# A two-layer hybrid decoder step with product-key experts: openings of PSUM banks, an inverse, sums of squares and the causal mixers rewritten with fewer and smaller products

## The chip, the cores and the metric

One of the eight cores of a Trainium2 chip runs the kernel. The metric is the device time of one launch in microseconds (us), from the first to the last instruction with what lies around them. All data is float32, in which TensorE (PE) runs each product as two records in the trace, a load of the stationary operand and a pass of the moving one each time. Transposes run as one.

## What is computed

A prompt of 256 tokens and 8 samples of one token (264 columns) go through two layers of the same form. `xn` is the normalised input.

```python
proj = xn @ w_in                        # 4 mixers' columns, then 4 x 1024 gate columns
y_a = rwkv7(proj)                       # per head a 64x64 state, delta rule
y_b = hgrn2(proj)                       # gated linear attention
y_c = retention(proj)                   # causal scores times a decay
y_d = mlstm(proj)                       # causal scores times exp(gates), with a normaliser
merged = sum(sigmoid(gates_m) * (y_m @ w_branch_m) for m in range(4))
x = x + merged @ w_out
q = rms_norm(x) @ peer_w_q              # 8 heads, two halves against 128 keys each
i1, i2 = top16(q1 . keys1), top16(q2 . keys2)
eidx, gate = top16 of the 256 sums, softmax     # 128 experts per token
x = x + sum(gate * gelu(u[eidx] . xn) * v[eidx])
```

Retention and mLSTM need for every head, with q, k and v of 64 channels, `att = (q k^T) * mask`, then `att v` and (mLSTM) the sums of the rows of `att`. RWKV-7 is done in chunks of 64 tokens: its update needs the inverse of `I + M` for each chunk and head, where `M` is strictly triangular, 64x64; there are 16 of them (4 chunks, 4 heads).

## The kernel before

The work is written out by hand for five engines, which meet at semaphores; the order on each engine is the order in the code. Channels lie on the partitions and tokens in the free dimension. Per layer:

- **Input products** (L503 to L551, `column_tile`): 32 column tiles of the mixers' part of `w_in`, 8 products of 128x128 by 264 columns each. HGRN2's own work (products `head_sum`, transposes, a scan) is set between them; after tile 25 comes its last sum into bank 6, opened and closed by a product of zeros (`nothing`) with 512 columns (L543, L551), which starts or ends the accumulation.
- **Mixers**: RWKV-7 first. `chunk_m` gets the chunks' matrices; the inverse (L651 to L663 on PE, L1431 to L1442 on VectorE, DVE) starts from the identity in `xx` and runs 6 rounds with blocks of 1, 2, 4 ... 32; each round is a product `T` (L654), a masking on DVE (`rr`), two products (L660, L662) and an addition. `open_y` (L640) opens the two banks of the outputs with 512 columns of zeros, L668 the bank of the states; then a chain of 4 chunks. Then retention and mLSTM by `causal(mixer, ...)` (L699 to L748), between them the two scalar gates of mLSTM (L757 to L760, `w_if`), once for each gate with 4 stationary columns.
- 32 **gate tiles** (`gate_products`, L566; again 8 products of 264 columns) are spread over the mixers as filling, by the constants `EARLY_GATES`, `GATES_AT` and others. Weights come in blocks of 1 MB (2 tiles) through four slots of `ring`, by SP's queue.
- **Branches, output projection** (`project`, L838) and query projection (L857). In `project`, DVE adds every block to `x` (L1642) and squares it (L1288); PE sums the squares over the partitions with a product by ones, two blocks later (`sum_square`, L485). ScalarE's root (L948), DVE's reciprocal and the norm follow.
- **Experts**: for each of 2 token tiles 128 gathers of 128 rows of 8 KB (POOL, L1262), for the samples 8. DVE makes the dot product (L1737), ScalarE the gelu and a diagonal matrix (L1171, L1173), PE the weighted sum (`weighted`, L893), into two banks that `open_sum` (L899) and `close_sum` (L903) open and close with 512 columns of zeros each. At the end ScalarE copies the sums (L1183), PE turns them, DVE adds them to `x`.

In `causal` PE transposes values and keys (L705), ScalarE copies them (`vpad`, `ktok`), POOL copies the keys of each head into `keyz` (L1226), which is zero in the other head's 64 rows, so that a product with all 128 rows (L714, L715) gives one head's scores:

```python
mm(bank(b, SEQ), keyz[:, mixer, q, pr, 0:P], q_[:, pr, 0:SEQ], start=True, stop=True)
mm(bank(b, P, SEQ), keyz[:, mixer, q, pr, P:SEQ], q_[:, pr, P:SEQ], start=True, stop=True).then_inc(S("pe_sc"), 1)
```

The values stand in `vpad` between 64 columns of zeros on each side, so that the products of both heads of a pair (L725, L727) add up in all 128 partitions of one bank. The sums of mLSTM's rows use `onespad` in the same way.

## Time and profile before

| | |
|---|---|
| median of 3 runs | 2353.87 us (2351.02 to 2362.21) |
| the profiled execution | 2362.78 us, its span 2360.7 us |
| mean granted TensorE clock | 0.933 |
| PE busy | 1984.7 us (84%) |
| DVE busy | 1418.6 us (60%) |
| ScalarE (ACT) busy | 583.7 us (25%) |
| GpSimd (POOL) busy | 651.4 us (28%) |
| moved by DMA | 665.61 MB, mean 282 GB/s |

The span runs from the first to the last instruction. The durations of a stretch are those of this one execution. The granted clock is a share of full speed (2.4 GHz); of a stretch it is a mean over its two levels, 1.2 and 2.4 GHz. "PEld" is PE's loading of stationary operands, which can run beside its passes. A shape such as "128*128 128x264" is stationary rows * columns, then what moves.

### The profile page before, as it was taken

What the parts mean: (1) busy time and instruction counts of PE and PEld (TensorE: products, weight loads), DVE (VectorE), ACT (ScalarE), POOL (GpSimd) and SP (SyncE); (2) the same over time, 40 slices, a digit from 0 to 9 for tenths busy, and PEclk for the clock granted to TensorE, in tenths of its full rate; (3) what the DMA queues carried; (4) which work ended last, traced back from release to release, by engine and by line L of the source; (5) the groups of instructions that cost most, each with busy time, mean ns of one, the idle gap of its engine ahead of it and who ended that gap; (6) DMA issues with size and microseconds to landing.
All of it is one profiled execution on the core that took longest, in us unless ns stands there. A gap on an engine that the chain in (4) does not pass through costs nothing.

```text
span 2360.7 us, 25431 instructions
## 1 busy us (share of the span) xinstructions
PE 1984.7 (84%) x7872; PEld 1176.3 (50%) x7872; DVE 1418.6 (60%) x3591; ACT 583.7 (25%) x1556; POOL 651.4 (28%) x668
## 2 busy tenths in 40 slices
PE   6999989997778877878889898899878878777887
PEld 5767677763333332323368677787433333333323
DVE  1425454458878777776533443644687786877755
ACT  1221222033222222222222203220332222322222
POOL 0400000024444444544213000000434444344441
PEclk9999989999888998899999999999988989898998
DMA  6330233559999999999853201433899999999995
GB/s 238 122 109 2 75 117 113 191 195 422 396 421 416 415 421 409 412 422 410 355 204 108 91 36 42 153 126 143 341 402 416 421 414 410 421 417 415 415 422 218
DMA packets 102051, 665.61 MB, mean 282 GB/s; under 512 B 20240, under 2 KB 21936, under 8 KB 21936
## 3 DMA queue, kind: packets, MB, share of 16 engines
q0 software_dynamic: 76032, 553.68, 57.0%
q1 hardware_dynamic: 24208, 107.12, 12.7%
q10 hardware_dynamic: 1696, 3.46, 0.4%
q8 instruction: 50, 0.82, 0.1%
q14 instruction: 65, 0.53, 0.1%
HBM read 657.64 MB, written 6.58 MB: 281 GB/s over the span
## 4 chain that ended last, share of the span: by engine, by line
PE 49%; DMA 26%; DVE 14%; issue 6%; ACT 3%; POOL 1%; SPq 0%; POOLq 0%; DVEq 0%; another core or an unknown queue 0%; ACTq 0%
DMA arena<-in_uv,arena 25%; PE ps L893 17%; PE ps L505 9%; PE ps L566 6%; PE ps L857 3%; PE ps L824 2%; PE ps L838 2%; DVE ring L1737 1%; PE ps L485 1%; ACT arena L1173 1%; POOL arena L1262 1%; PE ps L759 1%; PE ps L515 1%; DVE arena L1667 1%; DVE arena L1660 1%
## 5 line engine op out<-in xcount | busy, mean ns | idle before, releaser
L893 PE MATMUL ps<-ring,arena 128*128 128x512 f32 x1056 | 563.3, 688 | 224.9 <-ACT arena L1173 224.8
L893 PE MATMUL ps<-arena 128*128 128x512 f32 x1056 | 487.8, 602 | 46.6 <-ACT arena L1173 46.5
L893 PEld LDWEIGHTS ps<-ring,arena 128*128 128x128 f32 x1056 | 225.2, 221 | 560.4 <-ACT arena L1173 325.2
L1737 DVE SCALAR_TENSOR_TENSOR arena<-arena 128x1024 f32<-128x1024 f32 x264 | 323.3, 1225 | 222.3 <-DMA arena<-in_uv,arena 222.3
L1262 POOL DMA_INDIRECT ring<-in_uv,arena x264 | 296.5, 1123 | 469.4 <-PE ps L893 423.2
L1737 DVE SCALAR_TENSOR_TENSOR ring<-ring,arena 128x1024 f32<-128x1024 f32 x264 | 322.4, 1221 | 125.7 <-DMA ring<-in_uv,arena 91.4
L893 PEld LDWEIGHTS ps<-arena 128*128 128x128 f32 x1056 | 192.1, 189 | 334.7 <-issue 194.5
L1262 POOL DMA_INDIRECT arena<-in_uv,arena x264 | 273.2, 1035 | 247.2 <-PE ps L893 197.9
L1171 ACT ACTIVATE arena<-arena 128x1 f32<-128x1 f32 x528 | 107.1, 203 | 910.0 <-DVE ring L1737 487.8
L566 PE MATMUL ps<-xn,ring 128*128 128x264 f32 x1024 | 251.7, 406 | 15.7 <-ACTq L1122 9.3
L505 PE MATMUL ps<-xn,ring 128*128 128x264 f32 x1024 | 236.3, 391 | 6.0 <-DVE xn L1295 6.0
L566 PEld LDWEIGHTS ps<-xn,ring 128*128 128x128 f32 x1024 | 202.4, 200 | 55.6 <-issue 18.4
L1173 ACT ACTIVATE arena<-arena 128x128 f32<-128x128 f32 x528 | 212.5, 402 | 32.9 <-ACT arena L1171 2.0
L505 PEld LDWEIGHTS ps<-xn,ring 128*128 128x128 f32 x1024 | 196.3, 193 | 46.2 <-DVE xn L1295 6.9
L1738 DVE TENSOR_SCALAR arena<-const,arena 128x128 f32<-128x128 f32 x528 | 149.1, 282 | 0.0
L1252 POOL COPY arena<-arena 128x8 uint32 (+1 forms) x66 | 23.5, 356 | 402.6 <-DVEq L1716 402.3
L1226 POOL COPY keyz<-arena 64x512 f32<-64x512 f32 x8 | 4.9, 609 | 376.8 <-DVEq L1483 286.1
L967 ACT ACTIVATE arena<-ps 128x264 f32<-128x264 f32 x64 | 25.3, 395 | 224.8 <-PE ps L505 224.7
L1014 ACT ACTIVATE arena<-ps 128x264 f32<-128x264 f32 x50 | 19.6, 391 | 214.0 <-PE ps L566 213.7
L857 PE MATMUL ps<-xn,ring 128*128 128x264 f32 x256 | 61.1, 395 | 5.9 <-DVE xn L1295 5.9
L1236 POOL TENSOR_TENSOR arena<-arena 128x480 f32<-128x480 f32 (+14 forms) x30 | 28.3, 942 | 134.8 <-DVEq L1332 132.6
L824 PE MATMUL ps<-arena,ring 128*128 128x264 f32 x256 | 57.5, 387 | 2.0 <-remote 2.0
(391 smaller groups left out, 1794.9 us busy)
## 6 DMA issues: line engine op xcount, KB each, us to landing
ring<-in_w SPq DMA_DIRECT2D x88, 1024.0 KB, 4.9
ring<-in_uv,arena POOLq DMA_INDIRECT x264, 10.4
arena<-in_uv,arena POOLq DMA_INDIRECT x264, 14.0
st<-in_st SPq DMA_DIRECT2D x2, 2048.0 KB
out_st<-st SPq DMA_DIRECT2D x2, 2048.0 KB
const<-in_const ACTq DMA_DIRECT2D x1, 2729.0 KB, 11.5
arena<-in_keys SPq DMA_DIRECT2D x2, 1024.0 KB, 6.8
x<-in_x SPq DMA_DIRECT2D x1, 1056.0 KB, 5.2
```

Of the source, the lines that this page charges most:

```text
L505: m = mm(bank(b), ring[:, j, at:at + P], xn[:, kt, :], start=kt == 0, stop=kt == KT - 1)
L566: m = mm(bank(b), ring[:, j, at:at + P], xn[:, kt, :], start=kt == 0, stop=kt == KT - 1)
L824: m = mm(bank(b), ring[:, j, at:at + P], yy[:, 2 * m_ + k, :], start=k == 0, stop=k == 1)
L838: m = mm(bank(6 + o % 2), ring[:, j, at:at + P], src[:, kt, :], start=kt == 0, stop=kt == KT - 1)
L857: m = mm(bank(6 + o % 2), ring[:, o // 2, at:at + P], xn[:, kt, :], start=kt == 0, stop=kt == KT - 1)
L893: m = mm(bank(2 * tt + half, 512), dg[:, k, :], row(k)[:, D + 512 * half:D + 512 * half + 512], start=False, stop=False, skip_group_check= ...
L1171: own(act(hge[:, k:k + 1], hid[:, k:k + 1], ACT.Gelu))
L1173: act(dg[:, k, :], gd[:, k, :], ACT.Copy, scale=hge[:, k:k + 1]).then_inc(S("act_dg"), 1)
L1236: tt_(pairs[j], before[:, :, :, 1:], sub(HG + 2)[:, :, :, 1:SUB + 1 - j], ALU.mult).then_inc(S("pool_hg"), 1)
L1262: e.indirect_dma_start(out=row(k), out_offset=None, in_=A["uv"], in_offset=bass.IndirectOffsetOnAxis(ap=ix[:, par, k:k + 1], axis=0)).then ...
L1737: stt(u, u, 1.0, xtok[:, tt, :], ALU.mult, ALU.mult, accum_out=hid[:, k:k + 1]).then_inc(S("dve_hid"), 1)
L1738: ts(gd[:, k, :], C("ident"), gate, None, ALU.mult).then_inc(S("dve_hid"), 1)
```

## The change

1. **Openings.** The last sum of HGRN2 is opened by a product of zeros over 32 columns and closed by its own last product. `open_y` covers only the half of the columns which the following products don't write themselves. L668, `open_sum` and `close_sum` use one column, and `close_sum` one product instead of two.
2. **Inverse.** The first round, with blocks of 1, is `I` plus masked elements of `chunk_m`. DVE makes the transposed one by a masking with the new constant `level0` and an addition, PE turns it by a product with the identity (`channel`), DVE copies it. Five rounds follow.
3. **Causal mixers.** `keyz`, `vpad`, `onespad` and POOL's copies are gone. Scores of both heads of a pair are products over 64 rows each, `q = 0` and `q = 1` next to each other, into banks 6 and 7. Values lie dense in `vals`; the products with them have 64 stationary columns and write 64 partitions each.
4. **Scalar gates.** `w_if` gets 36 columns (4, 28 of zeros, 4), so that one pass makes both gates.
5. **Squares.** In `project` DVE adds up the eight squares itself, and PE makes one product by ones at the end.

The constants are 128 columns shorter. Input and output are the same otherwise.

```diff
@@ -540,7 +539,8 @@
                                        vexp[:, tt, h, :, :].rearrange("p c v -> p (c v)"), start=True, stop=True)
                         m.then_inc(S("pe_step"), 1)
                     if t == 25:
-                        mm(bank(6, 512), nothing, const[:, 0:512], start=True, stop=False, skip_group_check=True)
+                        mm(bank(6, 512).rearrange("p (a b) -> p a b", b=SEQ)[:, :, 0:SUB], nothing, nothing[:, 0:PR * SUB].rearrange("p (a b) -> p a b", b=SUB),
+                           start=True, stop=False, skip_group_check=True)
                         for c in range(1, NSUB):
                             e.wait_ge(S("dve_hs"), c)
                             for h in range(H):
@@ -548,7 +548,7 @@
                                 ch = slice(HD * q, HD * q + HD)
                                 m = mm(ps[ch, 6, pr * SEQ + c * SUB:pr * SEQ + c * SUB + SUB], hst[ch, pr, c - 1, :],
                                        eb[ch, pr, c * SUB:c * SUB + SUB], start=False, stop=False, skip_group_check=True)
-                        mm(bank(6, 512), nothing, const[:, 0:512], start=False, stop=True, skip_group_check=True).then_inc(S("pe_step"), 1)
+                        m.then_inc(S("pe_step"), 1)
                 e.wait_ge(S("sp_ln"), 16)
                 e.wait_ge(S("sp_par"), 16 * 8)
 
...
                 def open_y(u):
 
-                    mm(bank(1 + u, 512), nothing, const[:, 0:512], start=True, stop=False, skip_group_check=True)
+                    mm(bank(1 + u, 512).rearrange("p (a b) -> p a b", b=2 * CH)[:, :, chunk(1 - u)], nothing, bc(nothing[:, 0:CH], 1, [P, 4, CH]), start=True, stop=False, skip_group_check=True)
                     for tt in range(TT):
                         for h in range(H):
                             pr, q = divmod(h, 2)
@@ -647,14 +647,19 @@
 
                 open_y(0)
 
-                for k in range(6):
+                for tt in range(TT):
+                    e.wait_ge(S("dve_inv"), tt + 1)
+                    for h, u, on, n in heads_of(tt):
+                        m = mm(ps[on, 5 + tt, h * CH:h * CH + CH], xx[on, tt, 1, h, :], C("channel")[on, :], start=True, stop=True)
+                    m.then_inc(S("pe_p"), 1)
+                for k in range(1, 6):
                     for tt in range(TT):
-                        e.wait_ge(S("dve_inv"), max(2 * k + tt, 1))
+                        e.wait_ge(S("dve_inv"), 2 * k + tt + 1)
                         for h, u, on, n in heads_of(tt):
                             m = mm(ps[on, 3 + tt, h * CH:h * CH + CH], chunk_m[on, n, 0:CH], xx[on, tt, 0, h, :], start=True, stop=True)
                         m.then_inc(S("pe_t"), 1)
                     for tt in range(TT):
-                        e.wait_ge(S("dve_r"), 2 * k + tt + 1)
+                        e.wait_ge(S("dve_r"), 2 * k + tt - 1)
                         if k < 5:
                             for h, u, on, n in heads_of(tt):
                                 mm(ps[on, 5 + tt, h * CH:h * CH + CH], xx[on, tt, 1, h, :], rr[on, tt, h, :], start=True, stop=True)
@@ -664,8 +669,8 @@
 
                 e.wait_ge(S("act_step"), step("act_bv"))
                 open_y(1)
-                e.wait_ge(S("dve_inv"), 13)
-                mm(bank(6, 512), nothing, const[:, 0:512], start=True, stop=False, skip_group_check=True)
+                e.wait_ge(S("dve_inv"), 14)
+                mm(bank(6, 1), nothing, nothing[:, 0:1], start=True, stop=False, skip_group_check=True)
                 open_banks(7, 0)
                 for c in range(NCH):
                     tt, u = divmod(c, 2)
...
 
-                def causal(mixer, q_, k_tiles, v_tiles):
+                def causal(mixer, q_, k_, v_tiles):
 
 
                     e.wait_ge(S("dve_qk"), mixer + 1)
...
                     m.then_inc(S("pe_ctr"), 1)
                     close_banks(6, 7)
-                    e.wait_ge(S("pool_kz"), mixer + 1)
-                    for h in range(H):
-                        pr, q = divmod(h, 2)
-                        b = 6 + h % 2
-                        if h >= 2:
-                            e.wait_ge(S("dve_att"), 4 * mixer + h - 1)
-                        mm(bank(b, SEQ), keyz[:, mixer, q, pr, 0:P], q_[:, pr, 0:SEQ], start=True, stop=True)
-                        mm(bank(b, P, SEQ), keyz[:, mixer, q, pr, P:SEQ], q_[:, pr, P:SEQ], start=True, stop=True).then_inc(S("pe_sc"), 1)
+                    for pr in range(PR):
+                        if pr:
+                            e.wait_ge(S("dve_att"), 4 * mixer + 2)
+                        for q in range(2):
+                            mm(bank(6 + q, SEQ), k_[chunk(q), pr, 0:P], q_[chunk(q), pr, 0:SEQ], start=True, stop=True)
+                        for q in range(2):
+                            mm(bank(6 + q, P, SEQ), k_[chunk(q), pr, P:SEQ], q_[chunk(q), pr, P:SEQ], start=True, stop=True).then_inc(S("pe_sc"), 1)
                     e.wait_ge(S("act_cv"), mixer + 1)
                     e.wait_ge(S("dve_att"), 4 * mixer + 4)
                     e.wait_ge(S("dve_y"), 1)
-                    def over_keys(out, late, values):
-
-                        for q, tt in ((0, 0), (0, 1), (1, 1), (1, 0)):
-                            h = 2 * pr + q
-                            pad = HD - HD * q
-                            if tt:
-                                m = mm(late, values(tt, h, pad), att[:, h, SEQ:ATT], start=False, stop=False, skip_group_check=True)
-                            else:
-                                m = mm(out, values(tt, h, pad), att[:, h, 0:SEQ], start=q == 0, stop=q == 1)
+
+                    def over_keys(b, values):
+
+                        for pr in range(PR):
+                            for q in range(2):
+                                mm(ps[chunk(q), b + pr, 0:SEQ], values(0, 2 * pr + q), att[:, 2 * pr + q, 0:SEQ], start=True, stop=False)
+                            for q in range(2):
+                                m = mm(ps[chunk(q), b + pr, P:SEQ], values(1, 2 * pr + q), att[:, 2 * pr + q, SEQ:ATT], start=False, stop=True)
                         return m
 
-                    for pr in range(PR):
-                        m = over_keys(bank(pr, SEQ), bank(pr, P, P), lambda tt, h, pad: vpad[:, tt, h, pad:pad + P])
+                    m = over_keys(0, lambda tt, h: vals[:, tt, h * HD:h * HD + HD])
                     if mixer:
-                        a = CONST_AT["onespad"][0]
-                        for pr in range(PR):
-                            m = over_keys(bank(2 + pr, SEQ), bank(2 + pr, P, P), lambda tt, h, pad: const[:, a + pad:a + pad + P])
+                        m = over_keys(2, lambda tt, h: C("ones", HD))
                     m.then_inc(S("pe_co"), 1)
 
                     e.wait_ge(S("dve_kw"), mixer + 1)
...
                 causal(0, qr, kq, proj[:, RT + 4:RT + 6, :])
-                for g in range(2):
-                    for kt in range(KT):
-                        m = mm(ps[0:4, 2 + g, 0:N], w_if[:, kt, 4 * g:4 * g + 4], xn[:, kt, :], start=kt == 0, stop=kt == KT - 1)
+                for kt in range(KT):
+                    m = mm(ps[0:36, 2, 0:N], w_if[:, kt, :], xn[:, kt, :], start=kt == 0, stop=kt == KT - 1)
                 m.then_inc(S("pe_step"), 1)
...
                         m.then_inc(S(tag), 1)
-                        if o >= 2:
-                            sum_square(2, o - 2)
-                    for kt in range(KT - 2, KT):
-                        sum_square(2, kt)
+                    e.wait_ge(S("dve_sq"), KT + 1)
+                    mm(bank(2), C("ones"), sqs2[:, 0, :], start=True, stop=True).then_inc(S("pe_ss"), 1)
 
                 project(merged, "pe_wo", "dve_x")
 
...
                 def open_sum(tt):
                     for half in range(2):
-                        mm(bank(2 * tt + half, 512), nothing, const[:, 0:512], start=True, stop=False)
+                        mm(bank(2 * tt + half, 1), nothing, nothing[:, 0:1], start=True, stop=False, skip_group_check=True)
 
                 def close_sum(tt):
-                    for half in range(2):
-                        m = mm(bank(2 * tt + half, 512), nothing, const[:, 0:512], start=False, stop=True)
-                    m.then_inc(S("pe_acc"), 1)
+                    mm(bank(2 * tt + 1, 1), nothing, nothing[:, 0:1], start=False, stop=True, skip_group_check=True).then_inc(S("pe_acc"), 1)
...
                 e.wait_ge(S("act_step"), step("act_sv0"))
-                e.tensor_copy(xx.rearrange("p a b c d -> p (a b c) d"), bc(C("channel"), 1, [P, TT * 2 * H, CH])).then_inc(S("dve_inv"), 1)
-                for k_ in range(6):
+                for tt in range(TT):
+                    e.wait_ge(S("dve_cm"), 2 * tt + 2)
+                    own(tt_(xx[:, tt, 1, :, :], chunk_m[:, tt * H:tt * H + H, 0:CH], bc(C("level0"), 1, [P, H, CH]), ALU.mult))
+                    tt_(xx[:, tt, 1, :, :], xx[:, tt, 1, :, :], bc(C("channel"), 1, [P, H, CH]), ALU.add).then_inc(S("dve_inv"), 1)
+                for tt in range(TT):
+                    e.wait_ge(S("pe_p"), tt + 1)
+                    e.tensor_copy(xx[:, tt, 0, :, :].rearrange("p a b -> p (a b)"), bank(5 + tt, 256)).then_inc(S("dve_inv"), 1)
+                for k_ in range(1, 6):
                     lev = CONST_AT["levels"][0] + k_ * CH
                     for tt in range(TT):
-                        e.wait_ge(S("pe_t"), 2 * k_ + tt + 1)
+                        e.wait_ge(S("pe_t"), 2 * k_ + tt - 1)
                         tt_(rr[:, tt, :, :], bank(3 + tt, 256).rearrange("p (a b) -> p a b", b=CH), bc(const[:, lev:lev + CH], 1, [P, H, CH]), ALU.mult)\
                             .then_inc(S("dve_r"), 1)
                     for tt in range(TT):
...
-                    square(o, sqs2)
+                    own(tt_(sqs2[:, o, :], x[:, o, :], x[:, o, :], ALU.mult))
+                    if o:
+                        own(tt_(sqs2[:, 0, :], sqs2[:, 0, :], sqs2[:, o, :], ALU.add))
+                e.sem_inc(S("dve_sq"), 1)
 
                 norm(2, lambda kt: V("ln2", kt))
```

Three places show how the change moves instructions. Each row is an instruction with its line, output and inputs and, in brackets, the semaphores that it waits for; "x8" is eight alike in a row.

PE from the opening of the y banks to the first rounds of the inverse (`dve_inv` comes when DVE has finished `xx`, `dve_r` when it has masked `rr`), before:

```order
L640 MATMUL ps<-const 128x512
L645 MATMUL ps<-arena 64x64 x8
L654 MATMUL ps<-arena 64x64 [waits dve_inv]
L654 MATMUL ps<-arena 64x64 x7
L654 MATMUL ps<-arena 64x64 [waits dve_inv]
L654 MATMUL ps<-arena 64x64 x7
L660 MATMUL ps<-arena 64x64 [waits dve_r]
L660 MATMUL ps<-arena 64x64 x7
L662 MATMUL ps<-arena 64x64 x8
L660 MATMUL ps<-arena 64x64 [waits dve_r]
```

and in the changed kernel:

```order
L640 MATMUL ps<-const 128x4x64
L645 MATMUL ps<-arena 64x64 x8
L653 MATMUL ps<-const,arena 64x64 [waits dve_inv]
L653 MATMUL ps<-const,arena 64x64 x7
L653 MATMUL ps<-const,arena 64x64 [waits dve_inv]
L653 MATMUL ps<-const,arena 64x64 x7
L659 MATMUL ps<-arena 64x64 [waits dve_inv]
L659 MATMUL ps<-arena 64x64 x7
L659 MATMUL ps<-arena 64x64 [waits dve_inv]
L659 MATMUL ps<-arena 64x64 x7
L665 MATMUL ps<-arena 64x64 [waits dve_r]
L665 MATMUL ps<-arena 64x64 x7
```

The products T (L654) that began the first round are replaced by products with the identity from `const` (L653); then the second round's T (now L659) waits for DVE's copies.

PE in a causal mixer, from the scores to the products with the values (`dve_att` counts the heads that DVE has masked, `pool_kz` POOL's copy, `act_cv` ScalarE's), before:

```order
L714 MATMUL ps<-arena,keyz 128x256 [waits pool_kz]
L715 MATMUL ps<-arena,keyz 128x128
L714 MATMUL ps<-arena,keyz 128x256
L715 MATMUL ps<-arena,keyz 128x128
L714 MATMUL ps<-arena,keyz 128x256 [waits dve_att]
L715 MATMUL ps<-arena,keyz 128x128
L714 MATMUL ps<-arena,keyz 128x256 [waits dve_att]
L715 MATMUL ps<-arena,keyz 128x128
L727 MATMUL ps<-arena,vpad 128x256 [waits dve_y,dve_att,act_cv]
L725 MATMUL ps<-arena,vpad 128x128 x2
L727 MATMUL ps<-arena,vpad 128x256 x2
L725 MATMUL ps<-arena,vpad 128x128 x2
L727 MATMUL ps<-arena,vpad 128x256
```

and in the changed kernel:

```order
L717 MATMUL ps<-arena 128x256 x2
L719 MATMUL ps<-arena 128x128 x2
L717 MATMUL ps<-arena 128x256 [waits dve_att]
L717 MATMUL ps<-arena 128x256
L719 MATMUL ps<-arena 128x128 x2
L728 MATMUL ps<-arena,vals 64x256 [waits dve_y,dve_att,act_cv]
L728 MATMUL ps<-arena,vals 64x256
L730 MATMUL ps<-arena,vals 64x128 x2
L728 MATMUL ps<-arena,vals 64x256 x2
L730 MATMUL ps<-arena,vals 64x128 x2
```

POOL is not waited for any more. There were two waits for a masked head between the scores, one for each later head; now there is one, which asks for two heads, ahead of both later heads.

PE in the output projection, its last two blocks (`dve_x` counts DVE's additions to `x`, `dve_sq` its squares), before:

```order
L838 MATMUL ps<-arena,ring 128x264 [waits dve_x]
L838 MATMUL ps<-arena,ring 128x264 x7
L485 MATMUL ps<-arena,const 128x264 [waits dve_sq]
L838 MATMUL ps<-arena,ring 128x264 [waits dve_x]
L838 MATMUL ps<-arena,ring 128x264 x7
L485 MATMUL ps<-arena,const 128x264 [waits dve_sq] x3
```

and in the changed kernel:

```order
L837 MATMUL ps<-arena,ring 128x264 [waits dve_x]
L837 MATMUL ps<-arena,ring 128x264 x7
L837 MATMUL ps<-arena,ring 128x264 [waits dve_x]
L837 MATMUL ps<-arena,ring 128x264 x7
L840 MATMUL ps<-arena,const 128x264 [waits dve_sq]
```

The sums of squares between and behind the blocks (L485) are gone but for one at the end (L840).

## Rows read from the trace of the kernel before

**Rows 1.** Stretches: start:end, length, busy time (records) of each engine, clock, DMA share, GB/s.

```profile
165.00:402.00 237.00, 212.94 (x1628) 169.83 (x1628) 110.89 (x210) 60.19 (x122) 2.44 (x4) 0.92 0.22 75
272.00:303.00 31.00, 30.23 (x118) 24.57 (x117) 14.26 (x47) 11.49 (x28) 1.23 (x2) 0.83 0.10 35
...
517.00:1170.00 653.00, 521.31 (x1068) 210.25 (x1068) 486.72 (x1296) 181.66 (x550) 289.36 (x287) 0.91 1.00 414
```

**Rows 2.** Chain that ended last, by engine (the page).

```profile
PE 49%; DMA 26%; DVE 14%; issue 6%; ACT 3%; POOL 1%; SPq 0%; POOLq 0%; DVEq 0%; another core or an unknown queue 0%; ACTq 0%
```

**Rows 3.** In order of time (start, length, instruction xrecords), gates and the gate tiles after.

```profile
262.39 7.28 PE L759 MATMUL ps<-xn,w_if 128*4 128x264 f32 x32
...
271.81 19.75 PE L566 MATMUL ps<-xn,ring 128*128 128x264 f32 x80 [2.13 <-ACTq L1083]
...
1435.52 18.06 PE L566 MATMUL ps<-xn,ring 128*128 128x264 f32 x80 [2.13 <-ACTq L1083]
```

**Rows 4.** In order of time, end of the experts in layer 1.

```profile
1177.34 1.88 PE L903 MATMUL ps<-const 128*128 128x512 f32 x4
...
1179.26 1.08 ACT L1183 ACTIVATE arena<-ps 128x512 f32<-128x512 f32 x2 [2.82 <-PE ps L903]
```

**Rows 5.** In order of time, loads for the one-column products (L746) of mixer 1.

```profile
313.45 0.97 PEld L746 LDWEIGHTS ps<-const,arena 128*128 128x128 f32 x8
```

**Rows 6.** In order of time, openings of the y banks in layer 1.

```profile
202.15 2.07 PE L640 MATMUL ps<-const 128*128 128x512 f32 x2
...
224.23 1.12 PE L640 MATMUL ps<-const 128*128 128x512 f32 x2
...
225.29 0.68 PE L645 MATMUL ps<-arena 64*64 64x64 f32 x16
```

**Rows 7.** In order of time, first round of the inverse in layer 1.

```profile
200.60 0.68 DVE L1432 COPY arena<-const 128x1024 f32<-128x1024 f32 x1
...
204.86 0.31 PE L654 MATMUL ps<-arena 64*64 64x64 f32 x1
...
206.71 0.63 PE L662 MATMUL ps<-arena 64*64 64x64 f32 x16
207.18 0.63 PE L660 MATMUL ps<-arena 64*64 64x64 f32 x16
...
208.13 0.68 PE L654 MATMUL ps<-arena 64*64 64x64 f32 x16
```

**Rows 8.** In order of time, products and loads in half of the array.

```profile
121.12 3.65 PE L539 MATMUL ps<-arena 128*64 128x512 f32 x16
...
122.03 0.14 PEld L539 LDWEIGHTS ps<-arena 128*64 128x64 f32 x2 [0.29 <-issue]
...
167.57 0.78 PE L585 MATMUL ps<-arena,wa_up 64*128 64x264 f32 x1 [3.34 <-ACT arena L1021]
...
167.57 0.80 PE L586 MATMUL ps<-arena,wa_up 64*128 64x264 f32 x1
```

**Rows 9.** In order of time, mixer 1 (mLSTM) in layer 1.

```profile
303.16 0.69 PE L714 MATMUL ps<-arena,keyz 128*128 128x256 f32 x2
...
304.47 1.02 DVE L1491 TENSOR_TENSOR arena<-ps,arena 128x384 f32<-128x384 f32 x2
...
307.36 0.67 PE L727 MATMUL ps<-arena,vpad 128*128 128x256 f32 x2 [0.70 <-issue]
...
312.67 1.05 PE L741 MATMUL ps<-vpad,arena 128*128 128x128 f32 x8
```

**Rows 10.** In order of time, last blocks of the output projection in layer 1.

```profile
457.63 0.61 PE L485 MATMUL ps<-arena,const 128*128 128x264 f32 x2
...
461.64 1.86 PE L485 MATMUL ps<-arena,const 128*128 128x264 f32 x6
461.84 0.43 DVE L1642 TENSOR_TENSOR x<-x,ps 128x264 f32<-128x264 f32 x1 [3.11 <-PE ps L838]
...
463.54 0.48 ACT L948 ACTIVATE arena<-ps,const 128x264 f32<-128x264 f32 x1 [60.38 <-PE ps L485]
```

60 lines of the change are left out of this document (20 added, 40 removed).

## The prediction

> **What bounds the kernel now.** I read the stages first [rows 1], then the chain of waits [rows 2], then the order of time in the places that the change touches. Layer 1 is ahead of the experts up to 517 us and in them up to some 1180 [rows 1]; layer 2 repeats it. In the experts' stage the DMA share is 1.00 at 414 GB/s and PE is busy 521 of 653 us [rows 1]: the gathered rows set the time, and PE's work there counts only after the last gather. Ahead of the experts PE is busy 213 of 237 us in the mixers [rows 1], and PE and DMA (nearly all of it the gathers) lead the chain with 49% and 26% [rows 2]. The first gathers wait for PE's projections, so what PE saves ahead of them moves the whole stage of the experts earlier. So I look for products on PE's own path; work that moves to DVE costs only where PE waits for DVE.
>
> **The change part by part**, for one layer, in us. A product in f32 is two records in the trace; 40 products of 264 columns took 18.06 at full clock [rows 3], 0.45 each, so 512 columns cost 0.86. Two such (L903) and the hand-over took 1.92 [rows 4], which agrees. A product of one column still loads 128 weights: eight such loads took 0.97 [rows 5], so the two of a product make 0.24.
>
> *Banks opened by one column.* After column tile 25 two products of 512 columns go and one of 32 comes, in the middle of a run of PE work: 2 x 0.86 - 0.24 = **1.5**. The second opening of the y banks halves its columns (0.43), and the opening of the state bank (L668) falls to one column: 0.86 - 0.24 = 0.62; both stand on the path to the chunk chain [rows 6]: **1.05**. In the experts, four openings and closings between the token tiles cost PE some 3.4, but DMA is at 1.00 through the stage [rows 1] and covers them, so I cost their going at nothing: without that cover it would be worth up to 3.4. The last closing stands bare: two products from 1177.34, ScalarE starts at 1179.26 [rows 4]; one column in their place saves 1.72 - 0.24 = **1.5**. Bounds for a one-column product: 0.12 (one load seen, the other hidden) to 0.5 (nothing pipelined), so the three sites, 4.05 together, lie between 3.1 and 4.5.
>
> *Shorter inverse.* Six rounds become five; in place of the first stand two masked additions per token tile on DVE, a product by the identity on PE and a copy. The first round ran from 204.86 to 208.13 [rows 7], 3.27. DVE is free at 200.60, where its copy of 0.68 stood [rows 7]; four operations of 256 columns, each some 0.45 with its wait, end at 202.4, while PE is still at the y opening (202.15) [rows 6]: hidden. That opening ran at half clock (2.0 for one product), and half of it goes: 0.86. PE then reaches the new product at about 204.1, issues 16 records in 0.47 (206.71 to 207.18 [rows 7]), DVE copies in 0.43 (264 columns out of PSUM [rows 10]), and with two hand-overs of 0.2 round 1 starts at 205.4 and not at 208.13: **2.7**, and 2.3 in layer 2, where the opening ran at full clock. Bounds 1.5 to 3.3.
>
> *Causal mixers.* Out goes POOL's copy and the padding. A score product now has 64 rows and its neighbour the other 64. That such pairs run side by side is seen at L585 and L586: both start at 167.57 and take 0.78 and 0.80 [rows 8]. But DVE masks head by head, and the second pair now waits for both heads of the first, where before head 2 waited for head 0 alone. In mixer 1 the old order took 303.16 to 307.36 [rows 9]. In the new, DVE still starts at 304.47, masks two heads in 1.02, PE needs 0.65 and a hand-over of 0.3, DVE 1.1 more: 307.75, so **-0.4**. In mixer 0 POOL's copy no longer gates (0.3) and half-clock products pair up: between 0.6 and -0.1, I take 0.
>
> The products with the values run in columns 0 to 63 and 64 to 127 together. L539 has this form: 8 products of 64x512 took 3.65, where 8 x 0.86 = 6.9 would be serial [rows 8]. Mixer 1 has 16 of these, 8 of 256 columns (0.43) and 8 of 128 (0.215), 5.2 in all (307.36 to 312.67 = 5.3 [rows 9]); half goes, **2.6**. Mixer 0 has 8: **1.3**. Against this, the array now changes shape twice on the path per mixer. From L640 to L645, where it changes, 1.06 passed and 0.86 is the product [rows 6]: 0.2 each time, so **-0.8** for both mixers.
>
> A rule speaks against this step. The Trainium skill, "TensorE: Matmul & The Clock Gate", Part 3, says that a weight load overlaps a running product only where the row groups differ, and these neighbours share all rows. L539's neighbours share them as well: its loads of 64 columns, 0.14 for two, stand 0.43 apart with a product's record of 0.43 between, and nothing is added to 3.65 [rows 8]. By the row the step gives 3.9; by the rule 0.5 (rival B).
>
> *Gates in one pass.* 16 products of 264 columns become 8. They ran for 7.28 with PE alone on the path (ACT, DVE and the next gate tile wait for them) [rows 3]: half, **3.6**. The 36 stationary columns add nothing by the rows: 4 columns took as long per product (0.455) as 128 do (0.45).
>
> *Squares on VectorE.* A sum of squares stood after each block of the output projection from the third on. The blocks' period is 461.64 - 457.63 = 4.01 [rows 10], of which 0.445 is the sum. Five leave the path before the last block ends: 2.2. In the tail DVE squares (0.43) and now adds (0.43, 0.46 with its wait) before PE's one product. So ScalarE starts 2.2 - 0.46 = **1.75** before 463.54. DVE has 1.4 of work in a period of 3.56, so it does not become the bound.
>
> The sum for layer 1: 1.5 + 1.05 + 1.5 + 2.7 - 0.4 + 2.6 + 1.3 - 0.8 + 3.6 + 1.75 = 14.8; layer 2: 14.3 (inverse 2.3, mixer 0 -0.1); in all **29**. The profiled execution took 2362.8 us, so its like would take 2333.8; the runs' median is 2353.9, 0.4% below it, and I forecast 2353.9 - 29 = **2325 us**. The larger DMA of w_if and the lost memsets of POOL lie beside the start, and cost nothing.
>
> **Rivals.** A measurement of this kernel tells about 0.5% (12 us) from no change.
>
> *A: the clock gives part back.* The products that go kept the array filled. The granted clock is 0.92 in the mixers, 0.83 in 272 to 303 [rows 1], and the five gate tiles (40 products) after the gates' product took 19.75 in layer 1 and 18.06 in layer 2 [rows 3]: the same work, one stretch of it at 1.2 instead of 2.4 GHz. If the halved products run at half clock their gain is gone (3.9 per layer), the tiles after them cost 1.7 more in each layer, and one round of the inverse doubles (2.5): 8.1 a layer, 16 in all, 2341 us. For it: the opening before the inverse was at half clock already. Against: 64x64 products ran through the inverse with PE busy throughout, and the gates' product of only four columns is what stood before the slow tile, and becomes shorter. 12%. The Trainium skill, "TensorE: Matmul & The Clock Gate", Part 1, says that activity releases the throttle and idling brings it back; by that rule alone A's chance would be higher, but the rows of layer 1 and 2 differ with the same program.
>
> *B: the pairs of 64 columns do not pay.* Two neighbours share all rows of the array. If their weight loads can't go under the running product, each record costs a load more: 0.07 (0.14 for two) [rows 8], 48 records a layer, 3.4 of the 3.9 gained, 2332 us. Against it: L539's loads lie 0.14 in every 0.43 and the products still took 3.65. 6%. The rule named above would have it so.
>
> *C: the clock gains.* The low-activity product of four columns halves and the tile of layer 1 stays at full clock; with the cover of the openings between the token tiles paying too, 8 us more: 2317 us. 8%.
>
> *D: slower.* A's mechanism over the whole 237 us of the mixers. If the clock there fell from 0.92 to the 0.83 that 272 to 303 shows, PE-bound time grows by 0.92/0.83 - 1 = 11%, 26 a layer, 52 in all: 2354 - 29 + 52 = 2377 us. It decides from a mean of about 0.87 on (15 more a layer), and exceeds the 0.5% from 0.85. The removed products are some 13 of PE's 213 us there, too little to move the mean that far: 3%.
>
> **How the numbers follow.** The forecast has 70%, A 12%, B 6%, C 8%, D 3%, 1% for what I don't see. Small terms move the forecast by 4 either way, the gathers' share and the median by 4 more. Faster than 2342: forecast, B, C and half of A, 0.90; within 0.5%: the rest of A and what I don't see, 0.07; slower: 0.03. The range of 8 in 10 is 2312 to 2340: it takes in the bounds of the openings and the inverse, C, B and part of A.
>
> **What would show it.** Right: the period of the output blocks 3.56; the gates' product 3.6; values' products 2.6 in mixer 1; the inverse's first T product 2.7 earlier; ScalarE after the last gather's product 1.5 earlier; the experts' stage as long as before, 15 earlier in layer 1. Wrong: records of 64x256 at twice their length (A), or one after the other (B); more idle time of PE for DVE in the output projection; or a stage of experts that is longer or shorter by more than 3, which none of my terms gives.

## The result, and the profile after

| | before | after |
|---|---|---|
| median of the runs taken together, us | 2356.4 (8) | 2344.2 (8; 2340.1 to 2350.8) |
| ratio, 95% interval | | 0.9941 [0.9926, 0.9956] |
| profiled execution, us | 2362.8 | 2342.4 |
| its span, us; mean granted clock | 2360.7; 0.933 | 2340.4; 0.928 |

The change makes the kernel 14 us faster by the ratio and 12 by the medians, where 29 were forecast. 2344 lies above the range of 2312 to 2340. One of the eight runs of before, 2388, is a slow run, and the ratio leaves it out. The profiled execution of after stands 20 below that of before; the one of before was 6 slower than its median, the one of after 2 faster.

The first thing to read is where the 20 lie. These are stretches of before, cut at the first sum of squares of a layer and at the first product of a gathered row (columns as in [rows 1]; the third is from the chunk chain to the gates' product in layer 2):

```profile
15.90:517.60 501.70, 464.20 (x2821) 374.74 (x2821) 212.15 (x475) 104.47 (x219) 35.58 (x44) 0.95 0.33 117
1188.40:1676.10 487.70, 449.12 (x2820) 365.00 (x2820) 212.07 (x475) 104.48 (x220) 35.41 (x44) 0.98 0.34 122
...
1391.90:1426.10 34.20, 30.72 (x297) 24.10 (x296) 15.55 (x48) 3.58 (x9) 1.21 (x2) 1.00 0.25 95
```

The same stretches of after; ahead of the last two stands the experts' stage, which answers to the third of [rows 1]:

```profile
15.00:497.80 482.80, 437.86 (x2724) 358.81 (x2724) 214.59 (x483) 104.46 (x217) 33.14 (x40) 0.96 0.33 121
1168.90:1656.50 487.60, 443.42 (x2724) 362.23 (x2725) 214.62 (x483) 104.72 (x218) 32.99 (x40) 0.94 0.34 122
497.80:1151.00 653.20, 517.66 (x1062) 208.35 (x1063) 486.20 (x1294) 180.69 (x546) 285.64 (x287) 0.91 1.00 414
214.90:247.90 33.00, 28.24 (x297) 21.65 (x297) 15.37 (x48) 3.52 (x8) 0.00 (x0) 1.00 0.26 99
1370.80:1407.40 36.60, 31.84 (x297) 24.12 (x296) 15.38 (x48) 3.52 (x8) 0.00 (x0) 0.86 0.23 89
```

Layer 1 needs 18.9 less ahead of its experts, layer 2 only 0.1 less, though both layers run the same program. What differs is the granted clock: it goes from 0.95 to 0.96 in layer 1, and from 0.98 to 0.94 in layer 2. The clock has two levels, 1.2 and 2.4 GHz, so the time at the lower one is twice (1 - clock) times the length. Added up from the same view in slices of 0.5 us it was 51 and 24 before, and 39 and 54 after. A stretch at half clock costs half its length where PE is the path. Taking that off gives 476 for both layers of before, and 463 and 461 for those of after: 13 and 15 less, where the terms ahead of the experts made 13.3 and 12.8. This is an estimate, since PE need not be the path in all of it. By it the sum of the terms was right at an equal clock, and what is missing went with the clock.

The terms one by one, in order of time in after (start, length, engine, line, instruction):

```profile
197.45 1.15 PE L659 MATMUL ps<-arena 64*64 64x64 f32 x32
...
214.61 0.38 PE L673 MATMUL ps<-const 128*128 128x1 f32 x2
...
283.60 0.70 PE L717 MATMUL ps<-arena 64*128 64x256 f32 x4
...
286.08 0.70 PE L717 MATMUL ps<-arena 64*128 64x256 f32 x4 [1.56 <-DVE arena L1469]
...
288.15 1.12 PE L728 MATMUL ps<-arena,vals 128*64 128x256 f32 x4 [1.15 <-issue]
...
292.33 1.16 PE L741 MATMUL ps<-vals,arena 128*128 128x128 f32 x8
...
436.74 0.43 DVE L1620 TENSOR_TENSOR x<-x,ps 128x264 f32<-128x264 f32 x1 [2.19 <-PE ps L837]
...
440.30 0.43 DVE L1620 TENSOR_TENSOR x<-x,ps 128x264 f32<-128x264 f32 x1 [2.20 <-PE ps L837]
...
441.78 0.71 PE L840 MATMUL ps<-arena,const 128*128 128x264 f32 x2 [1.58 <-DVEq L1627]
...
442.53 0.48 ACT L943 ACTIVATE arena<-ps,const 128x264 f32<-128x264 f32 x1 [58.75 <-PE ps L840]
...
445.43 10.38 PE L854 MATMUL ps<-xn,ring 128*128 128x264 f32 x32 [2.94 <-DVE xn L1267]
...
1159.43 0.28 PE L899 MATMUL ps<-const 128*128 128x1 f32 x2
...
1159.74 1.08 ACT L1176 ACTIVATE arena<-ps 128x512 f32<-128x512 f32 x2 [1.22 <-PE ps L899]
...
1407.41 3.75 PE L758 MATMUL ps<-xn,w_if 128*36 128x264 f32 x16
```

The first product T of the inverse (L659) stands right behind the product by the identity; what the inverse is worth is read from its single edit below. The output projection has a period of 3.56 (436.74 to 440.30), and ScalarE follows the last block by 2.23 where it was 1.70 [rows 10]. PE now waits 1.58 for DVE ahead of the one sum of squares (L840), which it did not before: the prediction's sign of more idle time for DVE. The gates' product takes 3.75 for 7.28 [rows 3]. From the last closing to ScalarE it is 0.31 for 1.92 [rows 4]. In mixer 1 the scores took 4.55 (283.60 to 288.15) for 4.20 [rows 9], a loss of 0.35. The values' products there took 4.18 (288.15 to 292.33), not 2.6: the first four records take 1.12, and the same shape takes 0.65 at full clock, as shown next. The openings and the halved records are as forecast; the clock under them is not.

Mixer 0 shows it best. After, in order of time, first layer 1, then layer 2 (one program):

```profile
240.23 1.09 PE L710 MATMUL ps<-const,arena 128*128 128x128 f32 x8 [2.03 <-DVEq L1461]
241.25 0.70 PE L717 MATMUL ps<-arena 64*128 64x256 f32 x4
...
243.28 0.70 PE L717 MATMUL ps<-arena 64*128 64x256 f32 x4 [1.11 <-DVE arena L1469]
...
245.36 0.65 PE L728 MATMUL ps<-arena,vals 128*64 128x256 f32 x4 [1.15 <-issue]
...
246.81 1.16 PE L741 MATMUL ps<-vals,arena 128*128 128x128 f32 x8
...
1397.19 1.23 PE L717 MATMUL ps<-arena 64*128 64x256 f32 x4
...
1399.95 1.22 PE L717 MATMUL ps<-arena 64*128 64x256 f32 x4 [1.11 <-DVE arena L1469]
...
1402.75 1.12 PE L728 MATMUL ps<-arena,vals 128*64 128x256 f32 x4 [1.15 <-issue]
...
1405.51 1.98 PE L741 MATMUL ps<-vals,arena 128*128 128x128 f32 x8
```

At full clock the eight products with the values take 1.45 (245.36 to 246.81), near the forecast of 1.3; at half clock they take 2.76. Ahead of them PE waits three times, 2.03, 1.11 and 1.15. The first of the three is old; the other two were 0.29 and 0.70, as layer 2 of before shows:

```profile
1417.19 1.09 PE L705 MATMUL ps<-const,arena 128*128 128x128 f32 x8 [2.03 <-DVEq L1483]
1418.58 0.70 PE L714 MATMUL ps<-arena,keyz 128*128 128x256 f32 x2 [0.29 <-POOL keyz L1226]
...
1422.42 0.67 PE L727 MATMUL ps<-arena,vpad 128*128 128x256 f32 x2 [0.70 <-issue]
```

From the chain to the gates' product layer 1 takes 33.0 at clock 1.00 and layer 2 takes 36.6 at 0.86: more than the 34.2 that the long form took at full clock in layer 2 of before.

### The profile page after: what moved, and what is told of

Read it like the earlier page. It is cut to its first block, busy times and chain, and to the rows that moved or that the text cites. A ratio compares the mean times of both kernels' runs of the same rounds, so it can differ in the third digit from the quotient of the medians.

```text
span 2340.4 us, 25037 instructions
## 1 busy us (share of the span) xinstructions
PE 1944.0 (83%) x7668; PEld 1152.8 (49%) x7668; DVE 1425.1 (61%) x3607; ACT 583.7 (25%) x1552; POOL 635.8 (27%) x658
## 3 DMA queue, kind: packets, MB, share of 16 engines
q1 hardware_dynamic: 24208, 107.35, 12.8%
## 4 chain that ended last, share of the span: by engine, by line
PE 49%; DMA 26%; DVE 15%; issue 6%; ACT 3%; POOL 1%; SPq 0%; DVEq 0%; POOLq 0%; another core or an unknown queue 0%; ACTq 0%
DMA arena<-in_uv,arena 25%; PE ps L890 18%; PE ps L504 9%; PE ps L566 6%; PE ps L854 3%; PE ps L823 2%; PE ps L837 2%; DVE ring L1718 1%; ACT arena L1166 1%; PE ps L484 1%; POOL arena L1234 1%; PE ps L514 1%; DVE arena L1648 1%; DVE arena L1641 1%; DVE arena L1564 0%
## 5 line engine op out<-in xcount | busy, mean ns | idle before, releaser
L566 PEld LDWEIGHTS ps<-xn,ring 128*128 128x128 f32 x1024 | 202.9, 201 | 56.1 <-issue 18.6
L504 PEld LDWEIGHTS ps<-xn,ring 128*128 128x128 f32 x1024 | 196.5, 193 | 45.0 <-DVE xn L1267 6.8
L854 PEld LDWEIGHTS ps<-xn,ring 128*128 128x128 f32 x256 | 51.6, 203 | 16.1 <-DVE xn L1267 6.7
```

The source lines that it names most:

```text
L504: m = mm(bank(b), ring[:, j, at:at + P], xn[:, kt, :], start=kt == 0, stop=kt == KT - 1)
L566: m = mm(bank(b), ring[:, j, at:at + P], xn[:, kt, :], start=kt == 0, stop=kt == KT - 1)
L854: m = mm(bank(6 + o % 2), ring[:, o // 2, at:at + P], xn[:, kt, :], start=kt == 0, stop=kt == KT - 1)
```

## Experiments

**The theory.** T, made after the result: each part saves what its row gives at an equal clock; but the change takes away products that filled PE and shortens others, so PE idles for a larger share of the mixers, more stretches fall to half clock, and those take half of the gain. **The rivals.** R1 says that the parts are worth less than their rows (pairs that do not overlap, work behind a wait, DVE late), and the clock is chance. R2 says that idle time has nothing to do with it, and what counts is where instructions stand. In each recorded expectation R is the rival of that run alone.

"Clock" is the mean over the timed runs. The kernel before stood at 0.934 over 74 runs, the changed one at 0.926. Within one kernel the runs differ by up to 23 us, and a run's time follows its clock: over the runs of all kernels, each taken against its own kernel's mean, 0.001 of clock goes with 1.4 us (correlation -0.75). The column "at 0.930" moves each mean by that slope; it is a comparison, not a measurement. Each ratio is to the kernel before as it ran beside that kernel, and such groups of before had medians from 2357.9 to 2364.9.

| kernel | ratio to before, 95% | median us | clock | at 0.930 |
|---|---|---|---|---|
| before | | 2357.9 to 2364.9 | 0.934 | 2365.7 |
| openings only | 0.9964 [0.9946, 0.9982] | 2350.6 | 0.932 | 2352.0 |
| inverse only | 1.0001 [0.9980, 1.0023] | 2359.8 | 0.932 | 2362.2 |
| causal mixers only | 1.0009 [0.9989, 1.0030] | 2360.7 | 0.930 | 2360.9 |
| gates only | 0.9988 [0.9969, 1.0007] | 2354.7 | 0.932 | 2357.8 |
| squares only | 0.9986 [0.9965, 1.0008] | 2358.6 | 0.934 | 2365.3 |
| the whole change, again | 0.9940 [0.9917, 0.9963] | 2345.1 | 0.926 | 2338.7 |

### Each part alone, on the kernel before

Openings:

```diff
-                        mm(bank(6, 512), nothing, const[:, 0:512], start=True, stop=False, skip_group_check=True)
+                        mm(bank(6, 512).rearrange("p (a b) -> p a b", b=SEQ)[:, :, 0:SUB], nothing, nothing[:, 0:PR * SUB].rearrange("p (a b) -> p a b", b=SUB),
...
-                        mm(bank(2 * tt + half, 512), nothing, const[:, 0:512], start=True, stop=False)
+                        mm(bank(2 * tt + half, 1), nothing, nothing[:, 0:1], start=True, stop=False, skip_group_check=True)
```

> The kernel before with the openings and closings alone in their short form. Theory T (each part saves what its row gives where the clock is equal, and the two whole kernels differ by less because more stretches at 1.2 GHz fall into the later one): the terms are 4.05 a layer, 8.1 in all, so 2348 against 2356; in the trace ScalarE starts 1.5 earlier after the last gather's product. The removed 512-column products filled PE, so the time at half clock outside the experts may grow from the 79 us of the kernel before, by 3.4 for each stretch, 1.7 us of time each. Rival R (openings are worth less than their columns, since PE's stay at them was hidden by a wait): no change in time at the same granted clock.

Measured: 0.9964, some 8.5 us with an interval from 4 to 13, and clock 0.932. The full worth of the term is in the time, so R1 does not hold for this part. Inverse:

```diff
-                for k in range(6):
+                for tt in range(TT):
+                    e.wait_ge(S("dve_inv"), tt + 1)
...
+                for k in range(1, 6):
```

> The kernel before with the shorter inverse alone. T: 2.7 and 2.3, 5 in all, 2351 against 2356, at an unchanged clock. R (the two masked additions on DVE and the hand-overs cost as much as the round): within 1.5 of the kernel before.

Measured: no gain in time, but the interval, from 5 faster to 5 slower, would hold one of 4. From the products ahead of the inverse (L635's in before) to the chunk chain layer 2 took 22.4, and 24.6 in before: 2.1, with no time at half clock in either. So R1's reason is not there. The clock was 0.002 lower; where the gain went, if it did, this run does not show. Causal mixers:

```diff
-                        mm(bank(b, SEQ), keyz[:, mixer, q, pr, 0:P], q_[:, pr, 0:SEQ], start=True, stop=True)
+                        for q in range(2):
+                            mm(bank(6 + q, SEQ), k_[chunk(q), pr, 0:P], q_[chunk(q), pr, 0:SEQ], start=True, stop=True)
...
-                                m = mm(out, values(tt, h, pad), att[:, h, 0:SEQ], start=q == 0, stop=q == 1)
+                                mm(ps[chunk(q), b + pr, 0:SEQ], values(0, 2 * pr + q), att[:, 2 * pr + q, 0:SEQ], start=True, stop=False)
```

> The kernel before with the causal mixers alone on 64-row products and pairs of 64 columns. T: values' products halve (2.6 and 1.3 a layer), shape changes and the scores' wait take 1.2 a layer, so about 5 in all, 2351 against 2356; PE's busy time falls by some 8 in all, and where a mixer falls to half clock that layer gains nothing. R (the pairs do not run side by side): no gain, values' products 5.2 in mixer 1 as before, at full clock.

Measured: no gain in time, and the largest fall of the clock of all parts, to 0.930. Mixer 0 ran at full clock in both layers here, from the chain to the gates' product in 33.0 (34.2 in layer 2 of before), and from there to the output projection layer 2 took 163.7 (165.1), with the same 13.7 at half clock: 1.2 and 1.4, where the terms made 0.8 and 1.8. The pairs do run side by side. That would be 5 us in two layers, and the interval of the runs, from 3 faster to 7 slower, leaves it out. Mixer 1 of the same profile:

```profile
297.51 1.23 PE L710 MATMUL ps<-arena 64*128 64x256 f32 x4 [1.70 <-DVE arena L1461]
...
300.31 1.12 PE L721 MATMUL ps<-arena,vals 128*64 128x256 f32 x4 [1.15 <-issue]
...
303.97 0.61 PE L721 MATMUL ps<-arena,const 128*64 128x256 f32 x4
```

After waits of 1.70 and 1.15 PE's products take nearly twice their time. Before had 0.35 and 0.70 there (the second in [rows 9]): it issued its score products one head at a time, as DVE finished each. Gates:

```diff
-                for g in range(2):
-                    for kt in range(KT):
-                        m = mm(ps[0:4, 2 + g, 0:N], w_if[:, kt, 4 * g:4 * g + 4], xn[:, kt, :], start=kt == 0, stop=kt == KT - 1)
+                for kt in range(KT):
+                    m = mm(ps[0:36, 2, 0:N], w_if[:, kt, :], xn[:, kt, :], start=kt == 0, stop=kt == KT - 1)
```

> The kernel before with the gates' product in one pass alone. T: 3.6 a layer, 7.2 in all, 2349 against 2356; the product lasts 3.7 in place of 7.3 at full clock, and the gate tiles behind it take 18.1 or 19.8 by where a stretch at 1.2 GHz falls. R (the product is hidden: the wait behind it ends with something else): under 2 us in all.

Measured: 2.8 us by the ratio, with an interval from 7 faster to 2 slower, which holds both the 7 of T and R's less than 2. The product takes 3.75, and from it to the output projection layer 2 took 161.9 for 165.1 (13.7 at half clock in both): 3.2 of the 3.6. Squares:

```diff
-                        if o >= 2:
-                            sum_square(2, o - 2)
...
+                    e.wait_ge(S("dve_sq"), KT + 1)
+                    mm(bank(2), C("ones"), sqs2[:, 0, :], start=True, stop=True).then_inc(S("pe_ss"), 1)
```

> The kernel before with the squares of the output projection on VectorE alone. T: 1.75 a layer, 3.5 in all, at an unchanged clock; from the start of the output projection to the router's first product 33.9 in place of 35.5. But PE now waits for VectorE a little longer ahead of the router, so a stretch at 1.2 GHz may start there, which costs 1.7 a layer: then no gain in the runs and a mean clock lower by 0.002. R (VectorE's added work delays the projection): 35.5 or more at full clock.

Measured: 3.3, not told from none and not from the 3.5 either. From the output projection to the router it took 33.9 for 35.5 in both layers, 1.6 of the 1.75. From the router to the experts it took 51.0 and 51.1, where before took 51.1 in layer 1 and 49.4 in layer 2. So the half clock there is not the new wait's alone. Over all profiles with a bare router the count is plainer: its first tile ran partly at half clock in all 12 layers with the new squares, and in 6 of 10 with the old ones. The wait of 2.9 right ahead of the router is in all of them; that of 1.6 ahead of the sum of squares is new.

Three of the parts (inverse, causal mixers, squares) shortened their own place nearly as forecast and brought little or nothing that the runs can tell. Moved to an equal clock the five give 13.7, 3.5, 4.8, 7.9 and 0.4, together 30, and the whole change 27. The sum fits the forecast better than its parts do (8.1, 5.0, 5, 7.2 and 3.5), which the scatter may explain. This speaks for T, but a slope doesn't show a cause. The next runs do.

### Zero products in PE's idle time

Nine products of 512 columns by the zero weights are put into each layer, at three waits. Their results are not used.

```diff
+                    mm(bank(2, 512), nothing, const[:, 0:512], start=True, stop=True)
                     e.wait_ge(S("dve_sq"), KT + 1)
                     mm(bank(2), C("ones"), sqs2[:, 0, :], start=True, stop=True).then_inc(S("pe_ss"), 1)
+                    for _ in range(4):
+                        mm(bank(6, 512), nothing, const[:, 0:512], start=True, stop=True)
...
                     m = mm(bank(2, NS, NS * kt), xtok[:, 2, kt * P:kt * P + P], C("group"), start=True, stop=True)
                 m.then_inc(S("pe_xa"), 1)
+                for _ in range(4):
+                    mm(bank(5, 512), nothing, const[:, 0:512], start=True, stop=True)
```

> The changed kernel with zero products of 512 columns put into PE's idle time at three places: four where it waits for the sums of the layer's end (6.1 idle), one ahead of the sum of squares and four ahead of the router's first product (5.6 idle). None stands in time that PE needs. T (the time that the change did not bring is lost to half clock, and idle PE brings it on): the router's stretch and the layer's first products stay at full clock, some 10 less at half clock, so 5 faster than the changed kernel (2339 against 2344) and a mean clock 0.002 to 0.004 higher. R1 (the clock does not follow PE's idle time): same time and clock as the changed kernel. R2 (zero products delay what follows): slower by 1 to 4.

> The changed kernel as it is, beside the next three on one chip. Both theories: 0.994 of the kernel before, at a mean clock of 0.926. A median of 2344 to 2350, since the kernel before stood at 2365 in the runs beside a_fill and at 2358 in those before.

> The kernel of a_fill with its nine zero products cut to one column each: the same instructions in the same places, but nearly no columns in PE's idle time. T (columns in the idle time keep the clock up): no gain over a_same, within 2, at a clock of 0.926. R (a_fill gained by where its instructions stand, not by its columns): as fast as a_fill, 6 to 8 under a_same.

> a_fill once more beside a_same. T: 5 to 8 faster than a_same, by less half clock ahead of the router and at the start of layer 2, mean clock 0.928. R: the earlier gain was the chip's, and here the two are within 2.

| kernel | ratio to before, 95% | median us | clock |
|---|---|---|---|
| a_same: the changed kernel | 0.9940 [0.9917, 0.9963] | 2345.1 | 0.926 |
| a_one: nine products of one column | 0.9938 [0.9917, 0.9960] | 2344.4 | 0.926 |
| a_fill_b: nine of 512 columns | 0.9911 [0.9887, 0.9935] | 2339.0 | 0.930 |
| a_fill: the same kernel, other runs | 0.9893 [0.9868, 0.9918] | 2337.8 | 0.928 |

More work on PE makes the kernel 6 us faster (a_fill_b against a_same), and the same instructions without their columns don't: R2 falls. The intervals of the first and third row overlap; that the filled kernel came out faster in two sets of runs, and where the time comes from, speak for it all the same. In order of time, the output projection's end and the router's first tile, first in a_same:

```profile
446.61 0.71 PE L840 MATMUL ps<-arena,const 128*128 128x264 f32 x2 [1.58 <-DVEq L1627]
450.26 8.97 PE L854 MATMUL ps<-xn,ring 128*128 128x264 f32 x32 [2.94 <-DVE xn L1267]
```

and then in a_fill, where L839 and L843 are the zero products and L857 is the router:

```profile
444.58 1.02 PE L839 MATMUL ps<-const 128*128 128x512 f32 x2
446.32 0.71 PE L841 MATMUL ps<-arena,const 128*128 128x264 f32 x2 [0.72 <-DVEq L1632]
446.87 3.60 PE L843 MATMUL ps<-const 128*128 128x512 f32 x8
450.30 7.28 PE L857 MATMUL ps<-xn,ring 128*128 128x264 f32 x32
```

The router's first 16 products start 3.7 after the sum of squares in one (446.61 to 450.26) and 4.0 in the other (446.32 to 450.30), and take 8.97 and 7.28: the zero products cost 0.3 and bring 1.7. All 12 layers of the six profiles with these products have this tile at full clock, where the changed kernel's had it in none.

### More of them, in the mixers

Sixteen more a layer, in banks that nobody reads at the time:

```diff
+                for _ in range(3):
+                    mm(bank(2, 512), nothing, const[:, 0:512], start=True, stop=True)
                 e.wait_ge(S("act_step"), step("act_lr"))
...
+                take(e, bank_free[7], 1)
+                for _ in range(2):
+                    mm(bank(7, 512), nothing, const[:, 0:512], start=True, stop=True)
+                e.sem_inc(bank_free[7], 1)
                 causal(0, qr, kq, proj[:, RT + 4:RT + 6, :])
...
+                for _ in range(4):
+                    mm(bank(4, 512), nothing, const[:, 0:512], start=True, stop=True)
                 gate_tiles(GATES_AT[0])
```

> a_fill with sixteen more zero products of 512 columns a layer in PE's idle time in the mixers: three ahead of the low-rank products, one ahead of the sums of rk, two ahead of mixer 0's transposes, one after each pair of its scores, two behind the gates' product, four ahead of the gate tiles that wait for ScalarE after mixer 1, two ahead of the group means. T: the mixers' time at half clock (10.2 from the chunk chain to the gates' product and 20.5 from there to the output projection, a layer, in a_fill) falls to about half; some 15 a layer less at half clock, 7 a layer faster where all of it lies on the path, less where the zero products themselves delay what follows: 2325 to 2335. R (clock can't be had back in the mixers, or the zero products cost what they bring): within 3 of a_fill, or slower.

> a_fill2 with the two zero products ahead of the means' wait moved to the wait before it, where TensorE idles 2.0. T: they stood in TensorE's own time there (1.88 for two, a layer) and now don't: 2 to 4 faster than a_fill2 (2332): 2328 to 2330. R (they were covered): same as a_fill2.

> The changed kernel with zero products only around mixer 0: two of 512 columns ahead of its transposes (2.0 idle), one behind each pair of its scores (1.1 idle each). T: mixer 0 stays at full clock in both layers: from the chunk chain to the gates' product 33.0 in place of 36.6, so 5 to 7 faster than the changed kernel where both layers had it (2338 to 2340 against 2345 in the runs beside it). R (the half clock comes later in its place, and nothing is gained): within 2 of the changed kernel.

> The kernel before with the same zero products in the same idle times. T (the change brings new idle time on TensorE, and its half clock with it): the kernel before gains less than the change did (a_fill2 against a_same: 13), since its mixer 0 ran at full clock: 4 to 9, so 2351 to 2356 against 2360; the change's own worth with the clock held is then 20 to 28. R (both kernels gain alike from zero products, and the half clock has nothing to do with the change): 13 faster, 2347, and the change is worth 14 with them as without.

| kernel | ratio to before, 95% | median us | clock |
|---|---|---|---|
| a_fill2: with the mixers' waits filled | 0.9881 [0.9859, 0.9902] | 2332.1 | 0.938 |
| a_fill3: two of them moved to a real wait | 0.9830 [0.9802, 0.9857] | 2322.3 | 0.940 |
| a_m0: mixer 0 alone filled | 0.9898 [0.9874, 0.9922] | 2339.4 | 0.928 |
| b_fill: the kernel before, filled | 0.9929 [0.9904, 0.9953] | 2347.8 | 0.944 |

Mixer 0 settles the mechanism in one place. The stretch from the chain to the gates' product, in a_same, layers 1 and 2:

```profile
216.00:252.60 36.60, 31.83 (x297) 24.04 (x296) 15.38 (x48) 3.51 (x8) 0.00 (x0) 0.86 0.23 89
1376.30:1412.90 36.60, 31.84 (x297) 24.04 (x296) 15.37 (x48) 3.51 (x8) 0.00 (x0) 0.86 0.23 89
```

and in a_m0, whose only edit is four zero products there:

```profile
215.50:248.50 33.00, 32.06 (x305) 23.01 (x305) 15.38 (x48) 3.51 (x8) 0.00 (x0) 1.00 0.25 99
1370.40:1403.40 33.00, 32.06 (x306) 23.01 (x305) 15.38 (x48) 3.51 (x8) 0.00 (x0) 1.00 0.26 99
```

PE is busy for as long, 32, but now 3.4 of it are zeros, and the stretch is 3.6 shorter. Where both the short inverse and the short mixers are in and mixer 0 is bare, 9 of 10 layers in five profiles show 36.4 to 36.7 and one shows 33.0; with zero products in its waits all six layers of three profiles show 33. With the new mixers alone it was 33.0 in both layers, so they don't bring the half clock by themselves. Which other part it takes isn't shown: without the new mixers the stretch took 34.2 to 35.6, and 35.6 with the openings alone as with the inverse alone.

The gain is kept in the runs: a_m0 is 5.7 under a_same by the medians and 9.9 by the ratios to before, where its two stretches give 7.2. The two kernels didn't run side by side, and the intervals of their ratios just overlap, so the size is uncertain. A little may come later in its place, since the router to the experts took 52.2 and 52.5 for 51.0 in a_same.

a_fill3 was expected 2 to 4 under a_fill2 and came out 10 under by the medians. In order of time, the two that stood in no idle time in a_fill2 (L817; L820 waited for nothing):

```profile
350.37 1.88 PE L817 MATMUL ps<-const 128*128 128x512 f32 x4
352.09 1.94 PE L820 MATMUL ps<-arena,const 128*128 128x264 f32 x8
```

and where they stand in a_fill3, in a wait that was 1.97 and is now 0.91:

```profile
338.33 1.88 PE L810 MATMUL ps<-const 128*128 128x512 f32 x4
341.12 1.08 PE L813 MATMUL ps<-const,arena 128*128 128x32 f32 x8 [0.91 <-DVE arena L1591]
...
342.25 7.37 PE L566 MATMUL ps<-xn,ring 128*128 128x264 f32 x32
```

From the gates' product to the output projection a_fill3 took 161.6 and 163.1, where a_fill2 took 164.6 and 164.7. That is 3.0 and 1.6, so 4.6 of the 10. In layer 1 the gate tiles behind the wait also ran at full clock (7.37 for 9.05); in layer 2 they took 9.05 in both. The rest isn't explained, and may be the spread of the runs, which were not side by side. In this stretch a_fill2 fell short: its time at half clock went from 20.5 in a_same to 13.7 a layer, and the stretch did not get shorter (163.8 and 164.0 in a_same). The two misplaced products are part of why.

b_fill missed its expectation: the kernel before gains 16 from zero products, not 4 to 9, which is nearer to R's 13. It too lost time at half clock (51 and 24 ahead of the experts), and part of that comes back. So zero products help with or without the change, and the time at half clock is not the change's alone; the change has more of it.

What is the change worth, then, when both kernels are filled? Side by side they stand at 2347.8 and 2322.3, 25 apart by the medians and 23 by the means, give or take 5; unfilled it is 14. The comparison isn't quite equal. b_fill has 21 zero products a layer and a_fill3 has 25: b_fill lacks one between mixer 0's scores, the two ahead of the means and the one ahead of the sum of squares. Against a_fill2, which has the same 25 with two in the wrong place, b_fill is only 11 behind by the ratios. So 23 to 25 is what one pair of kernels shows. Their stretches ahead of the experts, b_fill first:

```profile
15.90:500.90 485.00, 459.05 (x2854) 368.60 (x2854) 212.09 (x475) 104.37 (x219) 35.62 (x44) 0.99 0.34 121
1174.00:1662.00 488.00, 461.94 (x2855) 370.37 (x2855) 212.21 (x475) 104.98 (x220) 35.49 (x44) 0.98 0.34 123
```

```profile
15.00:493.30 478.30, 450.25 (x2766) 361.91 (x2766) 214.65 (x483) 104.26 (x217) 33.12 (x40) 0.98 0.34 122
1163.60:1642.80 479.20, 451.72 (x2767) 363.52 (x2767) 214.49 (x483) 104.45 (x218) 32.98 (x40) 0.97 0.34 125
```

The second is a_fill3: 478 and 479 where the changed kernel took 483 and 488, with PE busy for 12 and 8 longer. By its runs it beats the kernel before by 1.7%. Zero products don't always pay where they raise the clock: from the gates' product to the output projection b_fill has 6.8 at half clock for the 13.7 in layer 2 of before, and takes 165.4 for 165.1.

### Without the inverse and the mixers

> The kernel before with openings, gates and squares of the change, without its inverse and its causal mixers. If parts add up as their single runs said (openings -7.4, gates -3.2, squares 0 to -3.5, inverse and mixers 0 to +2): 2345 to 2347, as fast as the whole change, at a mean clock above its 0.926. T says more: at equal clock the whole change would be 8 faster than this one, and in the runs the lower clock takes that back.

> The same with the zero products of the run a_fill in the three waits. T: 3 to 5 faster than without them, by a higher clock: 2341 to 2343. R1: no difference.

This kernel is the change without those two parts of the diff. Measured: 2345.8 (0.9929 [0.9907, 0.9951], clock 0.9305) without zero products and 2338.0 (0.9892 [0.9870, 0.9914], clock 0.935) with the nine of a_fill. The second gained 8 us where 3 to 5 were expected. So three parts of five are as fast as all five. By their own places the mixers are worth 5 us and the inverse 4; moved to an equal clock the whole change would be 8 faster than this kernel, and in the runs it isn't. With the same nine zero products both are at 2338. Whether the two parts pay once the mixers' waits are filled is not shown, since this kernel was not run with them filled.

## Why the prediction was wrong

- **Openings**, 8.1 in all: right (8.5 alone; 1.6 at the last closing for 1.5).
- **Shorter inverse**, 2.7 and 2.3: 2.1 in layer 2 of the single edit, at full clock. The product by the identity is 32 records and takes 1.10, where I read 16 records in 0.47.
- **Causal mixers**: the scores' loss of 0.4 is 0.35; the values' products take 1.45 in mixer 0, where before took 2.70 (1422.42 to 1425.12 in layer 2), and the whole mixer gives 1.2 and 1.4 for 0.8 and 1.8. L539's row was the right one to go by, and rival B falls: four products of 256 columns and four of 128 are 2.6 one after the other, and took 1.45. The Trainium skill ("TensorE: Matmul & The Clock Gate", Part 3) says that a weight load overlaps a running product only between different row groups. The 1.45, with all rows shared, does not agree with it.
- **Gates in one pass**, 3.6: 3.2 to 3.6. **Squares**, 1.75: 1.6.
- **The experts' stage**, "as long as before": from the first gathered row's product to the last it took 661.2 and 661.5, for 659.4 and 660.1. This took back the 1.6 a layer of the closing. It was 659.5 to 663.5 in the other kernels, without an order that I can name; this stays open. The openings between the token tiles, costed at nothing, show no gain here.
- **The step that failed** is the clock, which the sum of 29 put at nothing: every term was taken at the clock of its row, and A, which says that the clock gives part back, got only 12%. The runs showed in its place a mean clock of 0.926 for 0.934, 94 us at half clock ahead of the experts for 75 in the two profiles (some 9 us of time), 3.6 lost in mixer 0 in 9 of 10 layers, and 14 us gained for 29; with the waits filled in both kernels the gain was 23 to 25. The argument against A ("64x64 products ran through the inverse with PE busy") looked at where PE was busy. The half clock lay behind the places where it was not: after waits of 2.0, 1.1 and 1.2 ahead of mixer 0's products, of 1.6 and 1.2 ahead of mixer 1's, and of 1.6 and 2.9 ahead of the router. I had priced the longer waits (0.4) by their length alone. The 2.0 and the 2.9 are in the kernel before too, and its clock fell there in some layers; what the change does is to add to them.
- **A itself** stood at 2341, 3 off the measured 2344, and that is partly luck. It took the halved products of both mixers at half clock, 3.9 a layer; mixer 0's stretch alone lost 3.6, and in layer 1 the first products of mixer 1 with the values ran at half clock too. The gate tiles behind the gates' product, which it priced at 1.7 in each layer, were slow in layer 2 (19.75) and not in layer 1 (18.06). The inverse was slow in layer 2 alone, 22.4 for 20.9 from the products ahead of it to the chain. The router's first tile was slow in both, which A had not named. The Trainium skill ("TensorE: Matmul & The Clock Gate", Part 1) says that activity releases the throttle and idling brings it back. The runs with zero products agree (a_fill, a_m0), and I had set that rule aside for one pair of rows that differed between the layers.
- **C** wanted the gate tile of layer 1 at full clock. It was (18.06 for 19.75), and layer 2's went the other way, so nothing is gained.
- **D** kept the same mechanism and the wrong size: over the mixers the mean clock was 0.95 and 0.90 in the two layers, where it was 0.92 and 0.96, and not 0.83.
- **The base**: the median of the three runs shown was 2353.9, and that of 74 more was 2359.9. With that base the forecast would have been 2331, so some 6 of the 19 us between 2325 and 2344 are the base's and not the clock's.

## What to carry to other kernels

Where TensorE waits for another engine every few microseconds, a product that is taken out of it is worth its columns only if what is left keeps the clock. Sum the terms at full clock, then ask for every wait that the change makes longer or leaves bare what runs right behind it, and price that once at half clock. Zero products in real idle time, in banks that nobody reads, are a cheap test and, here, a cheap cure; put into time that PE needs, they cost their columns (1.9 for two). Run the kernel before with them too, since it may gain as well (16 us here). Compare kernels by their runs' clocks as well as by their times: a part with no gain in time can have its gain in place.

## What was unexpected of the hardware

One program's mixer 0 ran at 1.00 in layer 1 and at 0.86 in layer 2 of one execution, and the clock in that stretch turned from 0.86 to 1.00 in both layers by four products with zero weights. So here products with zero weights held TensorE's granted clock up as other work does, and a_one shows that it takes their columns. Runs of one kernel differ by 23 us (2349 to 2372 for the kernel before, beside these experiments), and they follow their mean clock, 0.001 with 1.4 us. The work is the same in all of them; whether the clock makes the time, or longer waits make both, this scatter alone doesn't show.
